# Expert rows of the second half: u and v of one token-slot gathered together, weighed two at a time, and summed with a diagonal stationary

## The reference

```python
def _peer(h, w_pq, sub_keys, peer_u, peer_v):
    qp = (h @ w_pq).reshape(b, s, PEER_HEADS, 2, PEER_HALF)          # 8 heads
    sc = einsum("bshpd,hpnd->bshpn", qp, sub_keys)
    s1, i1 = top_k(sc[..., 0, :], 16);  s2, i2 = top_k(sc[..., 1, :], 16)
    cand = s1[..., :, None] + s2[..., None, :]                       # 256 candidates
    top_s, top_c = top_k(cand, 16)
    expert = e1 * N_KEYS + e2;  gate = softmax(top_s)
    a = einsum("bcd,bchkd->bchk", h_c, peer_u[expert])
    w = gate * gelu(a)
    y = einsum("bchk,bchkd->bcd", w, peer_v[expert])
```

## Time and profile before

| | |
|---|---|
| median of three runs | 2506.24 us (2503.75 to 2518.59) |
| span of the profiled execution | 2607.5 us |
| PE busy | 2023.8 us, 78% |
| DVE busy | 1327.2 us, 51% |
| ACT busy | 503.5 us, 19% |
| POOL busy | 1076.8 us, 41% |
| moved by the gathers' queue | 564.84 MB, 56.8% of 16 DMA engines' span |
| mean granted TensorE clock | 0.85 |

### The profile page before, as it was taken

One profiled execution on the slowest core, in us unless ns is written; L12 is line 12 of the kernel. 1 busy time (PEld: TensorE's weight loads), 2 busy tenths in 40 slices (PEclk: granted clock), 3 DMA queues, 4 the chain that ended last, 5 costly groups with the idle time before them and its releaser, 6 DMA issues.

```text
span 2607.5 us, 26629 instructions
## 1 busy us (share of the span) xinstructions
PE 2023.8 (78%) x9392; PEld 1389.1 (53%) x9392; DVE 1327.2 (51%) x2969; ACT 503.5 (19%) x1204; POOL 1076.8 (41%) x1090
## 2 busy tenths in 40 slices
PE   8999999999889879998999999798723344423435
PEld 6888788886568757775777764455500000000001
DVE  5554110013238965557645359553776566575660
ACT  3312232012532221133110123322200000000000
POOL 2110000000004545545555445554576666667665
PEclk9999999989889979999999889789856556556667
DMA  7586334434239969998999989878999999999998
GB/s 281 180 325 210 106 129 153 154 121 139 83 140 347 391 228 380 387 393 313 392 386 405 374 299 345 310 283 337 351 359 388 381 372 357 381 355 387 350 377 320
DMA packets 214998, 780.08 MB, mean 299 GB/s; under 512 B 23923, under 2 KB 26547, under 8 KB 213843
## 3 DMA queue, kind: packets, MB, share of 16 engines
q0 software_dynamic: 155120, 564.84, 56.8%
q1 hardware_dynamic: 57560, 208.49, 22.2%
q10 hardware_dynamic: 2187, 5.05, 0.6%
HBM read 771.70 MB, written 6.58 MB: 298 GB/s over the span
## 4 chain that ended last, share of the span: by engine, by line
PE 62%; issue 13%; DVE 12%; another core or an unknown queue 4%; POOL 4%; DMA 3%; ACT 2%; ACTq 0%; SPq 0%; POOLq 0%; DVEq 0%
PE bank L637 47%; PE bank L901 5%; POOL main L570 3%; PE bank L835 2%; PE bank L853 2%; DVE main L1871 2%; DMA main<-in_peer_v,idx_v 1%; DVE dots L1871 1%; PE bank L844 1%; DVE ring L1871 1%; ACT main L1248 1%; PE bank L719 1%; DMA ring<-in_w_stream 1%; DVE best_v L1817 1%
## 5 line engine op out<-in xcount | busy, mean ns | idle before, releaser
L637 PE MATMUL bank<-main,ring 128*128 128x256 f32 x4864 | 1083.7, 383 | 16.8 <-ACT main L1248 4.3
L637 PEld LDWEIGHTS bank<-main,ring 128*128 128x128 f32 x4864 | 924.8, 192 | 176.9 <-issue 44.4
L570 POOL DMA_INDIRECT main<-in_peer_v,idx_v x512 | 518.6, 1013 | 438.0 <-PE bank L901 244.5
L901 PE MATMUL bank<-main,w_wide 128*32 128x512 f32 x2048 | 397.0, 797 | 308.0 <-issue 152.3
L570 POOL DMA_INDIRECT main<-in_peer_u,idx x427 | 440.4, 1031 | 343.1 <-DVE dots L1871 169.0
L901 PEld LDWEIGHTS bank<-main,w_wide 128*32 128x32 f32 x2048 | 81.3, 133 | 565.7 <-issue 564.3
L1871 DVE CUSTOM_DVE_ANT_0 main<-h_a,main 128x1024 f32<-128x1024 f32 x256 | 313.7, 1225 | 101.2 <-DMA main<-in_peer_u,idx 87.6
L1248 ACT ACTIVATE main<-bank 128x256 f32<-128x256 f32 (+3 forms) x304 | 124.3, 421 | 716.4 <-PE bank L637 582.1
L637 PE MATMUL bank<-ring,main 128*128 128x512 f32 (+3 forms) x624 | 239.6, 537 | 9.7 <-DMA ring<-in_w_stream 7.4
L1871 DVE CUSTOM_DVE_ANT_0 main<-bank,main 128x1024 f32<-128x1024 f32 x144 | 176.3, 1224 | 59.2 <-remote 26.4
L637 PEld LDWEIGHTS bank<-ring,main 128*128 128x128 f32 x624 | 109.5, 196 | 112.9 <-issue 96.1
(11 more groups left out here) (253 smaller groups left out, 1534.1 us busy)
## 6 DMA issues: line engine op xcount, KB each, us to landing
ring<-in_w_stream SPq DMA_DIRECT2D x372, 512.0 KB
main<-in_w_ada POOLq DMA_DIRECT2D x48, 512.0 KB, 9.1
main<-in_peer_v,idx_v POOLq DMA_INDIRECT x512
main<-in_peer_u,idx POOLq DMA_INDIRECT x427
main<-in_sub_keys SPq DMA_DIRECT2D x2, 1024.0 KB
main<-rows_d SPq DMA_DIRECT2D x1, 1536.0 KB
ring<-in_peer_u,idx POOLq DMA_INDIRECT x85
main<-in_xT ACTq DMA_DIRECT2D x1, 1024.0 KB, 5.4
```

Source lines behind the costliest of these rows:

```text
L570: gp.indirect_dma_start(rows_buf[slot], None, table, bass.IndirectOffsetOnAxis(ap=where, axis=0)).then_inc(landed[slot], 16)
L637: ins = pe.matmul(o, lhsT, rhs, **kw)
L901: last = mm(y_bank[half][s * CG:(s + 1) * CG, :], w_wide[:, lo:lo + CG], v_buf[slot][:, half * 512:(half + 1) * 512], start=q == 0, stop=q ...
```

## The change

The first half stays as it is through batch 57. In the second half:

- gather_uv(n) asks for the u row and the v row of the same slot with the same index column, one behind the other, into the two halves of an 8 KB slot, with one semaphore for both. 14 such slots take the room of the old u and v slots; the first 12 rows use only four of them, as the others are still in use by the first half or the dense work. Row 12 waits for batch 63 (v_used), row 16 for the end of dense(1). The turned indices, turned weights and widened weights of this half are gone, and with them the v order 40 rows behind.
- the held v rows go out before and between the first ten pairs, and batches 55 to 63 are combined within the pq stage of dense(1), as are the first five pairs of rows.
- row_dot works as dot did. After every second row DVE waits for ACT's gelu of these two dots and multiplies with the gates (row_weigh). The routing of the next head is done in five pieces behind the dots 4 to 8 of a head.
- ACT scales the 128 x 128 identity by the row's column of weights (a Copy activation with a scale per partition) into one of six diagonal tiles (DIAGS), which lie over a mask that is no longer needed.
- combine_rows(g): per row PE does two calls, diagonal 128 x 128 as stationary, the v half of the slot 128 x 512 as moving operand, added up in PSUM over the 128 rows of a tile; each row frees its slot (uv_used).

The core of the diff (the removed slot rules of u and v, renamed operands and the semaphores are left out; the constants are GROUP = 2, DIAGS = 6, UV_BUFS = 14):

```diff
+HELD = HALF_ROWS - V_HELD
+UV_NARROW, UV_FIRST, UV_BUFS, DIAGS = 4, 12, 14, 6
+GROUP = 2
+LIVE_HEADS = 4
+
+
+def uv_slot(n):
+
+    if n < UV_FIRST:
+        return n % UV_NARROW, n // UV_NARROW
+    q = n - UV_FIRST + UV_NARROW
+    k = q % UV_BUFS
+    return k, q // UV_BUFS + (UV_FIRST // UV_NARROW - 1 if k < UV_NARROW else 0)
+
+
+def uv_before(n):
+
+    if n < UV_FIRST:
+        return n - UV_NARROW if n >= UV_NARROW else None
+    return n - UV_BUFS if n - UV_BUFS >= UV_FIRST - UV_NARROW else None
...
+        uv_buf = ([region(U0 + 2 * i * D, 2 * D) for i in range(U_BUFS // 2)] + [region(V0 + 2 * i * D, 2 * D) for i in range(V_BUFS // 2)]
+                  + [ring[:, 2 * i:2 * i + 2, :].rearrange("p a b -> p (a b)") for i in range(2)]
+                  + [region(Z0, 2 * D)] + [region(F0 + 2048 + 2 * i * D, 2 * D) for i in range(3)])
...
+        diag = cst[:, 128:128 + DIAGS * P].rearrange("p (n c) -> p n c", n=DIAGS)
...
-            for hf in range(HALVES):
-                n0 = hf * HALF_ROWS
-                for m in range(HALF_ROWS):
-                    gather_u(n0 + m)
-                    for first, lag, count in ((n0 - V_HELD, HELD_FROM, V_HELD if hf else 0), (n0, V_LAG, HALF_ROWS)):
-                        i = m - lag
-                        if 0 <= i < count and i % N_CG == N_CG - 1:
-                            for s in range(N_CG):
-                                gather_v(first + i - (N_CG - 1) + s)
-                for n in range(HALF_ROWS - V_LAG, HALF_ROWS - (0 if hf else V_HELD)):
-                    gather_v(n0 + n)
...
+            def gather_uv(n):
+
+                t, j = TH + n // ROWS_PER_TILE, n % ROWS_PER_TILE
+                if j % TOPK == 0:
+                    gp.wait_ge(S["routed"], TH * HEADS + n // TOPK + 1)
+                if n == 0:
+                    gp.wait_ge(S["u_used"], HALF_ROWS)
+                if n == UV_FIRST:
+                    gp.wait_ge(S["v_used"], HALF_ROWS // N_CG)
+                if n == UV_FIRST + V_BUFS // 2:
+                    gp.wait_ge(S["lin_evacuated"], LIN[1]["end"])
+                before = uv_before(n)
+                if before is not None:
+                    gp.wait_ge(S["uv_used"], before + 1)
+                slot = uv_slot(n)[0]
+                gather(uv_buf[slot][:, 0:D], T["peer_u"], idx[:, t % 2, j:j + 1], uv_landed[slot])
+                gather(uv_buf[slot][:, D:], T["peer_v"], idx[:, t % 2, j:j + 1], uv_landed[slot])
+            for n in range(HALF_ROWS):
+                gather_u(n)
+                if n >= V_LAG and n % N_CG == N_CG - 1:
+                    for s in range(N_CG):
+                        gather_v(n - V_LAG - (N_CG - 1) + s)
+            for n in range(HALF_ROWS - V_LAG, HELD + 8):
+                gather_v(n)
+            for n in range(4):
+                gather_uv(n)
+            for n in range(HELD + 8, HELD + 16):
+                gather_v(n)
+            for n in range(4, 8):
+                gather_uv(n)
+            for n in range(HELD + 16, HELD + 20):
+                gather_v(n)
+            for n in range(8, 10):
+                gather_uv(n)
+            for n in range(HELD + 20, HALF_ROWS):
+                gather_v(n)
+            for n in range(10, HALF_ROWS):
+                gather_uv(n)
...
+            def combine_rows(g):
+
+                for n in range(GROUP * g, GROUP * (g + 1)):
+                    t, j = TH + n // ROWS_PER_TILE, n % ROWS_PER_TILE
+                    slot, fills = uv_slot(n)
+                    if n == 0:
+                        pe.wait_ge(S["wide_ready"], TH * HEADS)
+                    if n == ROWS_PER_TILE:
+                        pe.wait_ge(S["y_freed"], TH)
+                    pe.wait_ge(uv_landed[slot], 32 * (fills + 1))
+                    pe.wait_ge(S["diag_ready"], n + 1)
+                    for half in range(2):
+                        last = mm(y_of[t][half], diag[:, n % DIAGS, :], uv_buf[slot][:, D + half * 512:D + (half + 1) * 512],
+                                  start=j == 0, stop=j == ROWS_PER_TILE - 1)
+                    last.then_inc(S["uv_used"], 1)
...
                     if h == 0:
                         key_scores(0)
+                        if hf:
+                            experts_now[0].rest()
+                            experts_now[0] = None
                     if h >= 2:
                         key_scores(h - 1)
+                    if hf and h == 2:
+                        combine(HELD // N_CG)
+                        combine(HELD // N_CG + 1)
+                    if hf and h >= 3:
+                        combine_rows(h - 3)
+                    if hf and h >= 4:
+                        combine(HELD // N_CG + h - 2)
                 key_scores(HEADS - 1)
                 assert lin[0] == LIN[hf]["end"], (lin[0], LIN[hf]["end"])
                 mark("end")
             for hf in range(HALVES):
                 dense(hf)
-            experts_now[0].rest()
+            for g in range(HEADS - 3, HALF_ROWS // GROUP):
+                combine_rows(g)
...
+            def row_gates(h):
+
+                ac.wait_ge(S["least_ready"], h + 1)
+                m = h % LIVE_HEADS
+                ac.activation(gate_row[:, m, :], best_v[:, h % PH * TOPK:(h % PH + 1) * TOPK], ACT.Exp,
+                              bias=least[:, m:m + 1], accum_out=gate_sum[:, m:m + 1]).then_inc(S["row_exp"], 1)
+
+            def row_weights(g):
+
+                n = GROUP * g
+                h, j = n // TOPK, n % TOPK
+                m = h % LIVE_HEADS
+                if j == 0:
+                    row_gates(h)
+                d2 = dots_row[:, m, j:j + GROUP]
+                ac.wait_ge(S["row_dotted"], n + GROUP)
+                ac.activation(d2, d2, ACT.Gelu_apprx_tanh).then_inc(S["row_gelu"], 1)
+                ac.wait_ge(S["row_w_ready"], g + 1)
+                for i in range(GROUP):
+                    if n + i >= DIAGS:
+                        ac.wait_ge(S["uv_used"], n + i - DIAGS + 1)
+                    ac.activation(diag[:, (n + i) % DIAGS, :], ident, ACT.Copy, scale=w_row[:, m, j + i:j + i + 1]).then_inc(S["diag_ready"], 1)
...
+                    if hf and h >= 3:
+                        row_weights(h - 3)
...
+            def route_row(h):
+
+                yield from route(TH * HEADS + h)
+                best = best_v[:, h % PH * TOPK:(h % PH + 1) * TOPK]
+                st(ve.tensor_scalar(least[:, h % LIVE_HEADS:h % LIVE_HEADS + 1], best[:, 0:1], -1.0, None, ALU.mult), S["least_ready"])
+
+            def row_dot(n):
+
+                slot, fills = uv_slot(n)
+                t, h, j = n // ROWS_PER_TILE, n // TOPK, n % TOPK
+                h2 = h2_of(TH + t)
+                if n >= FROM_PSUM:
+                    ve.wait_ge(S["h2_copied"], 2 * TH)
+                    h2 = psum_all[:, t * D:(t + 1) * D]
+                ve.wait_ge(uv_landed[slot], 32 * (fills + 1))
+                u = uv_buf[slot][:, 0:D]
+                st(ve.tensor_tensor_reduce(out=u, in0=h2, in1=u, scale=1.0, scalar=0.0, op0=ALU.mult, op1=ALU.add,
+                                           accum_out=dots_row[:, h % LIVE_HEADS, j:j + 1]), S["row_dotted"])
+
+            def row_weigh(g):
+
+                h, j = GROUP * g // TOPK, GROUP * g % TOPK
+                m = h % LIVE_HEADS
+                if j == 0:
+                    ve.wait_ge(S["row_exp"], h + 1)
+                    st(ve.reciprocal(gate_inv[:, m:m + 1], gate_sum[:, m:m + 1]))
+                    if h >= LIVE_HEADS:
+                        ve.wait_ge(S["diag_ready"], TOPK * (h - LIVE_HEADS + 1))
+                ve.wait_ge(S["row_gelu"], g + 1)
+                st(ve.scalar_tensor_tensor(w_row[:, m, j:j + GROUP], dots_row[:, m, j:j + GROUP], gate_inv[:, m:m + 1],
+                                           gate_row[:, m, j:j + GROUP], ALU.mult, ALU.mult), S["row_w_ready"])
+
+            def rows_of_half():
+
+                heads = TH * HEADS
+                for _ in route_row(0):
+                    pass
+                routing = route_row(1)
+                for n in range(HALF_ROWS):
+                    h, j = divmod(n, TOPK)
+                    row_dot(n)
+                    if h and j == 4 and h + 2 <= heads:
+                        ve.wait_ge(S["row_exp"], h + 1)
+                        routing = route_row(h + 1)
+                    if j >= 4 or not h:
+                        next(routing, None)
+                    if j == TOPK - 1:
+                        for _ in routing:
+                            pass
+                    if n % GROUP == GROUP - 1:
+                        row_weigh(n // GROUP)
+                    if n == 24:
+                        finish(1)
+                        add_back(0)
+                        add_back(1)
+                    if n == ROWS_PER_TILE + 8:
+                        finish(TH)
+                        add_back(TH)
+                finish(TH + 1)
+                add_back(TH + 1)
```

167 lines of the change are left out of this document (68 added, 99 removed).

## The result

The changed kernel takes 2534.59 us (median of four runs, 2523.83 to 2540.54), the kernel before 2504.99 us over its four runs by then (2494.38 to 2518.59). The ratio is 1.0097 with an interval of 1.0062 to 1.0133: about 1% slower. The forecast was 2522 in a range of 2492 to 2558.

The account below looks back on a forecast made before the run. The prediction took PE to bound the dense work and gathers the tail, already at its floor in ordinary runs. Steady state 0, seam 10 + 2 and end 4 gave +16 us: 2506 + 16 = 2522 us, range 2492 to 2558.

Parts of the forecast that it names:

- What bounds the kernel, and the reading of the 101 us: PE bounds dense work, gathers the tail; the tail's lost 75 us belong to the profiled execution, 101 us above the median.
- The pauses: Tail stretches where DVE idles and gathers stop: 75 us lost in the profiled execution, taken as absent from ordinary runs.
- The floor: Fastest pitch of the tail's gathers, from an undisturbed stretch at 411 GB/s: 1.276 us per gather of 512 KB.
- Steady state 0: Second-half tail: same gathers and bytes, so no change if no engine needs more than 2.55 us a row.
- POOL waiting on nothing: Sign for the steady state: in an undisturbed tail stretch POOL never waits and pairs come every 2.5 to 2.6 us.
- The seam, +10 and +2: From pq stage to tail: eight more gathers left, +10 us, and slower PE pairs, +2 us.
- 29.3 of work, 12 of waits, 3 for the clock: PE time added to the pq stage: batches and row pairs, waits of 7 and 5 us, some half-clock work; end near 1913.
- The end, +4: Last landing to kernel end: a longer chain of 12 us instead of 8, so +4 us.
- DVE, 36.3 of 40.8 us: Tail: DVE needs 36.3 us a head against 40.8 us of gathers, 11% of air, so it does not bind.
- The 1.4 us at a head's first pair: DVE term in the tail: 1.4 us added per head for table loads of exp and gelu.
- PE, 1.78 us and a clock above 0.70: Tail: a row takes PE 1.78 us at full clock against 2.55; PE is no bound if the clock stays above 0.70.
- Sum: Whole kernel: seam 10 + 2 and end 4 give +16 us, 2522 us in the runs, 0.6% slower.

Follow-up runs that it names:

- e0: The kernel before the change, unchanged, profiled once more: span 2512.6 us, median 2514.64 us, ratio 1.0028.
- e2: Changed kernel with batch 57 one head later and, in heads 4 to 7, the held batch ahead of the pair of rows: 2524.84 us, ratio 1.0095.
- e4: Changed kernel with one more 128 x 1024 DVE operation behind each pair's first dot from row 16 on: 2573.37 us, ratio 1.0286.
- e8: Changed kernel with a third PE call for each row from row 16 on, except a tile's first and last: 2540.68 us, ratio 1.0124.
- e7: The changed kernel, unchanged, profiled once more: span 2537.9 us, median 2540.87 us, ratio 1.0154.
- e3: Changed kernel with one of a row's two PE calls left out, except a tile's first and last row: 2532.87 us, ratio 1.0107.
- e10: Changed kernel with pairs behind the pq stage, held batches reordered, last two rows single, two slots already free in that stage: 2522.05 us, ratio 1.0028.

## Why the prediction was right or wrong

- *What bounds the kernel, and the reading of the 101 us.* Right in kind: e0 shows the old tail without its pauses, at 1.287 us a gather, so nothing was there to be gained. The pauses cost 63 us and not 75 (480 gathers in 680 us, against 1.287 us for each); 31 us of the difference lay ahead of the pq stage. The floor was 1.276 by the stretch and is 1.287 in the whole tail.
- *Steady state 0.* Right, but for 1 to 3 us. The sign "POOL waiting on nothing" did not hold: it waits 24 us for the routing of heads, which the transfers in flight cover.
- *The seam, +10 and +2.* Right in its mechanism, too small in size: 14 gathers and 18 us instead of 12. The stage grew by 52 us (69.8 to 121.8), where the prediction added 44 to its end (29.3 of work, 12 of waits, 3 for the clock) and priced 2 more for slow pairs apart. The missing 6 us are the waits of the four pairs of heads 4 to 7 for their diagonals, 4 x 1.42 us, which it put at nothing; with them and part of batch 57's wait covered, e2 has 8 gathers less to go. That 121 us was forecast for the stage and 122 measured is luck: the forecast counts from the stage of the exceptional execution, which was 6 us longer than in e0. The 480 gathers left before agree with e0's 479 when both are counted from the end of the stage.
- *The end, +4.* From the last landing to the end 11.9 against 7.8 us, +4.1 as forecast. Nearly 2 us more lie ahead of that: the last issue to the last landing took 14.7 us (2495.42 to 2510.13) instead of 13.0 in e0; why is not shown.
- *DVE, 36.3 of 40.8 us.* Sign right, size off: the terms given add up to 36.05, and by e4 it is at most 34.5. The 1.4 us at a head's first pair are too many: behind the exp and gelu of a new head DVE waited 0.17 us in one trace.
- *PE, 1.78 us and a clock above 0.70.* 1.72 (2 x 0.86), clock 0.92 to 0.93 in the tail. e8 shows that half as much work again would hardly have been waited for. The rule of the Trainium skill (TensorEngine Tiling (Array Packing), Theoretical Speedup), up to four times the speed with 32 columns, held for PE's own time: 3.6 times as much for four rows (4 x 1.72 against 1.92).
- *Sum.* 18 + 2 + 6 = 26 instead of 16 us: 2506 + 26 = 2532, beside 2534.6 measured. The forecast that it stays near 1% slower was right, within its range, with a sum that was 10 us too small; whether it is inside or outside 1% the intervals leave open (0.6 to 1.3% at first, 1.1 to 2.0% for e7).

## What to carry to other kernels

Where a tail is bound by transfers, the work on every engine behind it is free until it uses up its air (here some 6.7 of 41.2 us on DVE, a call a row on PE); what a rewrite of the loop costs is decided at the loop's two ends, by how many transfers can be asked for before the loop runs freely and by the chain behind the last landing. Work that moves into a dense stage brings its waits along: count one for every place where it stands behind what it needs. Joining two buffers into one ties the release of both to the later reader: count the slots that can be filled while that reader is busy elsewhere. And before a difference is read from a profile whose span is far from the timed runs, profile that kernel once more; here even a stage ahead of the slow stretches was longer in it, 75.8 instead of 69.8 us.

## What was not expected of the hardware

- One execution of the kernel before took 2607.5 us, and in its tail short DVE operations had gaps of 0.7 us that wait for nothing shown, at a DMA share of 1.03. Its page puts 4% of the chain that ended last on "another core or an unknown queue", and POOL waits 46 us for such a releaser in 1915 to 2580. None of the twelve other profiles has such a tail or names such a releaser in that chain. The cause stays open.
- TensorE with 128 x 128 stationaries, kept busy 454 of 600 us, was granted 0.92 of its 2.4 GHz; with 590 of 600 0.99, with 336 of 600 0.74; with the strips of the kernel before, 221 of 610, 0.61. At its lower level of 1.2 GHz (0.50) a row would take an estimated 2 x 1.72 = 3.4 us, and PE would have been the bound. The tails of e3 and of the kernel before, whose means lie between the two levels, were there for part of the time; in both PE waited for gathers.
- Gathers alone ran at 408 to 409 GB/s over some 600 us in the tails that they bound (e0, the changed kernel, e3, e7, e8, e10). The Trainium skill (DMA: Bandwidth & Descriptors, Specifications) gives 358 GB/s of HBM per core, a stack's bandwidth divided by two cores; here one core ran, and the measurement decides.
